# Front of a hybrid encoder kernel: six PSUM banks for projection outputs, evictions ahead of weight splits, split first transfers, and a gather of h with the norm's factor in the selection

## The chip, the cores and the metric

The kernel runs on one core of a Trainium2 chip. Its time is device microseconds of the whole execution; the time of a version is the median over runs, each with its own launch. TensorE is PE below (its weight loads are PEld), VectorE is DVE, ScalarE is ACT, GpSimd is POOL, and SyncE (SP) issues nearly all DMAs.

## The reference

One layer on 256 frames of width 1024, float32:

```
hn   = rmsnorm(h, g_mix);  proj = hn @ w_in            # 1024 -> 2048: u | B | C | v, 512 each
pool = (trailing mean of u over 2/4/8/16 frames - u) @ w_pool[g] * pool_scale
conv = B * causal_conv3(C * v)
h    = h + concat(pool, conv) @ w_out
h    = h + attention(rmsnorm(h, g_xattn) -> q, rmsnorm(mem, g_mem) -> k, v; 4 heads of 256) @ w_o
hn   = rmsnorm(h, g_moe);  logits = hn @ w_router + b_router
h    = h + sum over the top 4 of 32 experts e:
           gate * (((clip(lin) + 1) * swiglu(hn @ w_gate_up[e] + b)) @ w_down[e] + b)
out  = rmsnorm(h, g_final)
```

The expert weights are 12 MB for each of 32 experts; every expert is read.

## The kernel before

**Two parts.** The *front* is everything up to the routing; the *expert loop* follows. In the front each product is made of three passes in float32r: a weight chunk of 1 MB (`ring`, eight places) is taken as two *halves* of 128x1024; for half j ACT writes `w_hi[j % 4]` (`hi(j)`, a rounding copy), DVE writes `w_lo[j % 4]` (`lo(j)`, the remainder), and PE multiplies hi by hi, hi by lo and lo by hi. Both `hi(j)` and `lo(j)` wait until PE has finished half j-4 (`halves_used`). `project_rows` (w_v, w_out, w_o) is 12 matmuls of 128x512 for a half and puts its four row tiles in PSUM banks 2 to 5; `project_columns` and `project_u` (w_in, w_k, w_q) are 24 matmuls of 128x256 for a half.

**The order of the front** is written out by hand for each engine. PE: transposes of mem; w_v (halves 0 to 7, with the transposes of the normed x after the fifth and the seventh); u0, u1 (8 to 11), C0 (12, 13), v0 (14, 15), pool frames 0, C1 (16, 17), v1 (18, 19), pool product 0, pool frames 1, B0 (20, 21), pool product 1, B1 (22, 23); w_out (24 to 31); k0 to k3 (32 to 39); q0 to q3 (40 to 47) with the scores, the transposes of the probabilities (`turn_probs`) and the products with v (`attend`); w_o (48 to 55, `project_head`); transposes of h and the logits.

**Banks.** All outputs of columns, pool, keys, queries, scores and heads go through banks 0 and 1 in turn, in the order of the list `A_USES`; use n waits until use n-2 was evicted. Who evicts: u, C, the frames' differences d, the queries and the first copy of a head are ACT's, each behind the `hi` pair that stands before it; `conv_in(i)` on DVE multiplies v by C (`z_pad`) and then does six tap instructions, `pool_out(i)` four instructions (`mix_hi`, `mix_lo`), `gate_conv(i)` three, `keys_out(c)` one. Banks 6 and 7 serve transposes.

**The start.** ACT issues six small transfers of gain rows into `vec_rows`; PE transposes all 48 rows at once into `vec` before it transposes mem.

**The experts.** Eleven *slots* of 2 MB (`SLOT_ORDER`) hold the weights, six chunks for each expert: four of w_gate_up, two of w_down. The first eleven are loaded as the front gives up its memory, the last of them after the logits (`lg_full`). Chunk n from the twelfth on is issued by SP only when PE has used chunk n-10 counted from one (`chunks_used`). For expert s, PE multiplies the rows of the normed tokens `n_rows` (written by ACT at L981, columns reordered so that k of 8 goes with p) by the 0/1 matrix `sel` (`gather`), ACT copies the result to `xg_sb`, PE transposes it in four pieces (`turn_tokens`), DVE applies `gain_moe` (`tokens_out`), and then come gate_up, the activation, its transposes (`turn_act`, which read every fourth column), down and scatter. `add_back` adds the result to `h_rows`. `keep_clock(n)` is n matmuls of the identity with itself.

## Time and profile before

| | us |
|---|---|
| median of 3 runs | 1146.5 (1143.35 to 1148.73) |
| profiled execution, its own time | 1145.61 |
| its span | 1143.9 |
| PE busy | 1076.5 (94%) |
| DVE, ACT busy | 342.6, 197.7 |
| chain that ended last, PE / DMA / DVE | 63%, 25%, 8% |

The profiled execution lies 0.9 us under the median, and its span 1.7 us under its own time. The page cuts the span in 40 slices; from the tenth to the last but one the DMA engines move 426 to 430 GB/s, ahead of that less. Busy PE is no sign that PE is the limit: matmuls are pipelined, and what a stage waits for has to be read from its waits.

### The profile page before, as it was taken

To read this page: it belongs to the slowest core of one execution; us is meant where nothing else is said; L and a number is where in the kernel's file an instruction comes from. 1 tells how busy PE (TensorE), PEld (TensorE's weight loads), DVE (VectorE), ACT (ScalarE), POOL (GpSimd) and SP (SyncE) were. 2 spreads that over 40 slices of the span, in tenths; PEclk is the share of its full clock that TensorE was granted. 3 is DMA by queue.
4 is the path that set the end of the run, shared out by engine and by line. 5 is a ranking of instruction groups with operands and counts; after the bars stand their busy time and mean duration, and the time that the engine had idled before them with its cause. 6 is when DMAs were issued, how large, how long until landed. Compare 5 with 4: busy or idle time off the path is not lost.

```text
span 1143.9 us, 12842 instructions
## 1 busy us (share of the span) xinstructions
PE 1076.5 (94%) x5419; PEld 489.2 (43%) x5420; DVE 342.6 (30%) x573; ACT 197.7 (17%) x323; POOL 26.1 (2%) x53
## 2 busy tenths in 40 slices
PE   8979999999999999999999999999999989999995
PEld 7978997733333333333333333333332333333332
DVE  8555645312222222222222222222222212222223
ACT  6523544400000000000000110100000000000002
POOL 6200000000000000000000000000000000000000
PEclk9999999899999999999999999999999999999998
DMA  9964555789999999999999999999999999999993
GB/s 351 349 212 146 170 221 229 286 365 428 427 426 427 430 427 427 427 429 427 427 426 429 428 428 426 429 427 428 427 429 426 428 427 428 429 427 426 429 429 156
DMA packets 52007, 437.94 MB, mean 383 GB/s; under 512 B 5184, under 2 KB 23024, under 8 KB 27376
## 3 DMA queue, kind: packets, MB, share of 16 engines
q1 hardware_dynamic: 51856, 437.10, 92.0%
q8 instruction: 45, 0.74, 0.3%
q14 instruction: 10, 0.08, 0.0%
q10 hardware_dynamic: 96, 0.02, 0.0%
HBM read 435.47 MB, written 1.05 MB: 382 GB/s over the span
## 4 chain that ended last, share of the span: by engine, by line
PE 63%; DMA 25%; DVE 8%; ACT 2%; issue 1%; ACTq 0%; DVEq 0%
PE ps L734 26%; DMA slot<-in_w_gate_up 25%; PE ps L768 14%; PE ps L476 7%; PE ps L534 6%; PE ps L779 3%; PE ps L752 2%; DVE glu L1338 2%; DVE lin L1335 2%; DVE glu L1331 2%; DVE lin L1332 1%; ACT sig L824 1%; PE ps L499 1%; PE ps L723 1%; ACT w_hi L824 1%
## 5 line engine op out<-in xcount | busy, mean ns | idle before, releaser
L734 PE MATMUL ps<-slot,xT 128*64 128x512 f32 x2048 | 456.9, 595 | 17.2 <-DMA slot<-in_w_gate_up 16.4
L734 PEld LDWEIGHTS ps<-slot,xT 128*64 128x64 f32 x2048 | 142.0, 136 | 310.4 <-issue 266.1
L768 PE MATMUL ps<-slot,sig 128*64 128x512 f32 x1024 | 226.8, 595 | 8.0 <-ACT sig L824 8.0
L1344 DVE TENSOR_TENSOR h_rows<-ps,h_rows 128x1024 f32<-128x1024 f32 x64 | 75.4, 1219 | 368.3 <-PE ps L779 368.3
L768 PEld LDWEIGHTS ps<-slot,sig 128*64 128x64 f32 x1024 | 70.7, 137 | 143.6 <-issue 127.9
L995 ACT ACTIVATE sig<-glu 128x512 f32<-128x512 f32 x32 | 20.2, 632 | 546.3 <-DVE glu L1331 546.3
L1331 DVE TENSOR_SCALAR glu<-ps 128x512 f32<-128x512 f32 x32 | 22.1, 692 | 280.1 <-PE ps L734 280.1
L1093 DVE TENSOR_TENSOR w_lo<-ring,w_hi 128x1024 fp32r<-128x1024 f32 x56 | 68.2, 1225 | 74.7 <-ACT w_hi L824 74.6
L824 ACT ACTIVATE xg_sb<-ps 128x512 f32<-128x512 f32 x65 | 38.9, 598 | 245.3 <-PE ps L768 230.0
L824 ACT ACTIVATE w_hi<-ring 128x1024 fp32r<-128x1024 f32 x56 | 59.0, 1062 | 83.8 <-PE ps L476 52.3
L779 PE MATMUL ps<-xg_sb,g_sb 64*128 64x512 f32 x256 | 63.6, 615 | 0.7 <-ACT xg_sb L824 0.7
L708 PE MATMUL ps<-n_rows,sel 128*64 128x512 f32 x264 | 64.0, 607 | 0.0
L779 PEld LDWEIGHTS ps<-xg_sb,g_sb 64*128 64x128 f32 x256 | 22.0, 186 | 41.8 <-issue 40.2
L752 PE MATMUL ps<-ident,glu 128*128 128x128 f32 x128 | 23.9, 309 | 13.7 <-DVE glu L1338 13.7
L1325 DVE TENSOR_TENSOR xT<-ps,gain_moe 128x512 f32<-128x512 f32 x33 | 22.8, 691 | 44.3 <-PE ps L716 44.3
L708 PEld LDWEIGHTS ps<-n_rows,sel 128*64 128x64 f32 x264 | 19.2, 139 | 37.8 <-issue 37.7
L476 PE MATMUL ps<-hn_hi,w_hi 128*128 128x256 f32 x160 | 23.1, 287 | 6.9 <-DVEq L1166 3.1
L752 PEld LDWEIGHTS ps<-ident,glu 128*128 128x128 f32 x128 | 17.8, 208 | 23.2 <-DVE glu L1338 23.2
L824 ACT ACTIVATE sig<-ps 128x512 f32<-128x512 f32 x32 | 19.1, 598 | 31.9 <-PE ps L752 31.9
L476 PEld LDWEIGHTS ps<-hn_hi,w_hi 128*128 128x128 f32 x160 | 20.6, 191 | 8.1 <-DVEq L1166 3.3
L1335 DVE SCALAR_TENSOR_TENSOR lin<-lin,glu 128x512 f32<-128x512 f32 x32 | 22.1, 691 | 1.3
L1338 DVE TENSOR_TENSOR glu<-lin,sig 128x512 f32<-128x512 f32 x32 | 22.1, 692 | 1.1
(190 smaller groups left out, 708.8 us busy)
## 6 DMA issues: line engine op xcount, KB each, us to landing
slot<-in_w_gate_up SPq DMA_DIRECT2D x128, 2048.0 KB, 36.4
slot<-in_w_down SPq DMA_DIRECT2D x64, 2048.0 KB, 37.5
ring<-in_w_in SPq DMA_DIRECT2D x8, 1024.0 KB, 13.9
ring<-in_w_v SPq DMA_DIRECT2D x4, 1024.0 KB, 10.6
ring<-in_w_out SPq DMA_DIRECT2D x4, 1024.0 KB, 12.1
ring<-in_w_k SPq DMA_DIRECT2D x4, 1024.0 KB, 5.7
ring<-in_w_q SPq DMA_DIRECT2D x4, 1024.0 KB, 5.2
ring<-in_w_o SPq DMA_DIRECT2D x4, 1024.0 KB, 4.8
```

The lines of the kernel that those rows point to most:

```text
L476: mm = pe.matmul(bank[:, (j % 2) * SEQ:(j % 2 + 1) * SEQ], w[:, k, :], src[:, k, :], start=(n == 0 and k == 0), stop=(n == 2 and k == KC - 1),
L534: mm = pe.matmul(ps[:, bank_row[r], :], src[:, k, t * P:(t + 1) * P], w[:, half * HALF:(half + 1) * HALF], start=(n == 0 and k == 0), stop ...
L708: mm = pe.matmul(ps[CAP * half:CAP * (half + 1), bank_xg, :], sel[:, t, :], n_rows[:, t, half * HALF:(half + 1) * HALF], start=(t == 0), s ...
L734: mm = pe.matmul(ps[CAP * half:CAP * (half + 1), bank, :], lhsT, w[:, a * CHUNK + bank * D + half * HALF:a * CHUNK + bank * D + (half + 1) ...
L752: mm = pe.transpose(ps[:, bank_t[1], j * P:(j + 1) * P], act[:].rearrange("s (p r) -> s r p", r=4)[:, j, :], ident[:])
L768: mm = pe.matmul(ps[CAP * half:CAP * (half + 1), bank_y, :], lhsT, w[:, r * D + half * HALF:r * D + (half + 1) * HALF], start=False, stop= ...
L779: mm = pe.matmul(ps[:, (4 if t == 0 else 2) + half, :], g_sb[rws, t * P:(t + 1) * P], y_sb[rws, :], start=True, stop=True, skip_group_chec ...
L824: act_e.activation(dst, src, ACT.Copy).then_inc(done, 1)
L1093: dve.tensor_tensor(w_lo[j % LO_BUFS][:].rearrange("p (k n) -> p k n", **shape), src, w_hi[j % HI_BUFS][:].rearrange("p (k n) -> p k n", * ...
L1331: dve.tensor_scalar(glu[:], ps[:, 0, :], LIMIT, None, ALU.min).then_inc(glu_ok, 1)
L1335: dve.scalar_tensor_tensor(out=lin[:], in0=lin[:], scalar=1.0, in1=glu[:], op0=ALU.add, op1=ALU.mult).then_inc(step_link, 1)
L1344: dve.tensor_tensor(h_rows[:, t, :].rearrange("p (a n) -> p a n", a=2), ps[:, b:b + 2, :], h_rows[:, t, :].rearrange("p (a n) -> p a n", a ...
```

## The change

**Banks.** `A_BANK` gives each output one of six banks, 0 to 5; banks 2 to 5 are shared with the row tiles, so `FIRST_AFTER_ROWS` adds waits for the evictions of w_v and w_out, and the row products wait for the last use of their bank. **Order.** On ACT and DVE evictions move ahead of splits; the six taps of `conv_in` become `conv_taps`, which stands behind one more `lo`. **Start.** The gain of mem has its own small transfer and its own transpose, issued first; the other five are transposed after the third half of w_v. The first chunk of w_v comes in two transfers. DVE prepares 16 columns of the pooling band and no longer 256, POOL fills the rest. **Experts.** ACT's write of `n_rows` goes; `gather` reads `h_rows` with `sel_rstd`, which is `sel` times the factor of the norm, one DVE instruction of 128x128 more for each expert. The reordering of columns moves into the transposes of `xg_sb` (every fourth column) and into which rows of w_gate_up a chunk holds: 16 KB in a row for each partition as before, but 32 KB from partition to partition instead of 64 KB. `acc` is a sum apart from `h_rows`.

```diff
-A_USES = ["u0", "u1", "C0", "v0", "d0", "C1", "v1", "pool0", "d1", "B0", "pool1", "B1", "k0", "k1", "k2", "k3",
-          "q0", "q1", "s0", "q2", "s1", "q3", "s2", "s3", "o0", "o1", "o2", "o3", "logits"]
+A_BANK = dict(u0=0, u1=1, C0=2, v0=3, d0=0, C1=4, v1=5, pool0=1, d1=0, B0=2, pool1=3, B1=0, k0=1, k1=0, k2=2, k3=3,
+              q0=4, q1=5, s0=0, q2=1, s1=2, q3=3, s2=4, s3=5, o0=0, o1=1, o2=0, o3=1, logits=0)
+A_USES = list(A_BANK)
+FIRST_AFTER_ROWS = {"C0": 0, "v0": 1, "C1": 2, "v1": 3, "k2": 0, "k3": 1, "q0": 2, "q1": 3}
...
+def a_uses(bank, upto):
+
+    return sum(A_BANK[n] == bank for n in A_USES[:A_USES.index(upto) + 1])
...
+        acc, out_rows = n_rows, h_rows
...
+        def a_evicted(eng, name):
+
+            eng.wait_ge(a_free[A_BANK[name]], a_uses(A_BANK[name], name))
...
             if c < GATE_UP:
-                return w_gate_up[0, bass.ds(e, 1), :, :].rearrange("o (p k) n -> p (o k n)", k=KC)[:, BIG * c:BIG * (c + 1)]
+                rows_of = w_gate_up[0, bass.ds(e, 1), HALF * (c // 2):HALF * (c // 2 + 1), :].rearrange("o (p a) n -> p (o a) n", a=4)
+                return rows_of[:, 2 * (c % 2):2 * (c % 2 + 1), :].rearrange("p a n -> p (a n)")
...
+                if q == 0:
+                    sp.dma_start(dst[:, 0:1, :], src[:, 0:1, :]).then_inc(first_half_in, 16)
+                    dst, src = dst[:, 1:2, :], src[:, 1:2, :]
                 sp.dma_start(dst, src).then_inc(slot_full[q % FRONT_RING], 16)
...
                 project_rows("w_v", k, mn_hi, mn_lo)
+                if k == 2:
+                    pe.wait_ge(vec_in, 16 * 5)
+                    bank, done = t_begin("vec")
+                    pe.transpose(bank[:, 0:N_ROWS], vec_rows[:], ident[0:N_ROWS, 0:N_ROWS]).then_inc(done, 1)
...
             def gather(s):
-                pe.wait_ge(sel_ok, s + 1)
+                pe.wait_ge(sel_rstd_ok, s + 1)
...
-                        mm = pe.matmul(ps[CAP * half:CAP * (half + 1), bank_xg, :], sel[:, t, :],
-                                       n_rows[:, t, half * HALF:(half + 1) * HALF], start=(t == 0), stop=(t == TC - 1),
+                        mm = pe.matmul(ps[CAP * half:CAP * (half + 1), bank_xg, :], sel_rstd[:, t, :],
+                                       h_rows[:, t, half * HALF:(half + 1) * HALF], start=(t == 0), stop=(t == TC - 1),
...
             hi(1, 2, 3)
+            t_out("vec", lambda bank, done: copy(vec[:, 0:N_ROWS], bank[:, 0:N_ROWS], done))
+            act_e.wait_ge(t_free[1], t_use("vec")[1])
...
-            hi(16, 17)
+            hi(15, 16)
             a_out("C0", c_buf[:])
-            hi(18, 19)
+            hi(17, 18, 19)
             a_out("d0", dT[:, 0:2, :])
...
-            act_e.wait_ge(rstd_ok, 1)
-            for c in range(TC):
-                act_e.activation(n_rows[:, c, :].rearrange("t (k p) -> t k p", p=P),
-                                 h_rows[:, c, :].rearrange("t (p k) -> t k p", p=P), ACT.Copy,
-                                 scale=stat[:, 3, 2, c:c + 1]).then_inc(scaled, 1)
...
-            lo(16, 17, 18, 19)
-            conv_in(0)
-            lo(20, 21, 22, 23)
-            conv_in(1)
+            lo(16, 17, 18)
+            conv_product(0)
+            lo(19)
+            conv_taps(0)
+            lo(20, 21, 22)
+            conv_product(1)
+            lo(23)
             dve.wait_ge(bias_split, 2 * PARTS - 1)
             pool_out(0)
-            lo(24, 25)
+            lo(24)
+            conv_taps(1)
             gate_conv(0)
+            lo(25)
             pool_out(1)
-            lo(26, 27)
+            lo(26)
             gate_conv(1)
...
-            largest(0), lo(48, 49)
-            scale_probs(0), largest(1), lo(50)
-            turned(0), lo(51), scale_probs(1)
-            largest(2), largest(3), scale_probs(2), scale_probs(3)
+            largest(0), lo(48), scale_probs(0), lo(49)
+            largest(1), turned(0), scale_probs(1), lo(50, 51)
+            largest(2), scale_probs(2), largest(3), scale_probs(3)
...
+            def normalise_selected(s):
+
+                dve.wait_ge(sel_ok, s + 1)
+                rstd = stat[:, 3, 2, :].unsqueeze(2).broadcast_to([P, TC, CAP])
+                dve.tensor_tensor(sel_rstd[:], sel[:], rstd, ALU.mult).then_inc(sel_rstd_ok, 1)
```

What the change moves on ACT at the start, in the stage of w_v: these are its instructions from the first gain copy to the squares of mem, before:

```order
L824 ACTIVATE vec<-ps 128x48
L851 ACTIVATE mn_hi_61<-ps,vec 128x256 x4
L824 ACTIVATE w_hi0_89<-ring_49 128x1024
L851 ACTIVATE mn_hi_61<-ps,vec 128x256 x4
L824 ACTIVATE w_hi1_90<-ring_49 128x1024
L824 ACTIVATE w_hi2_91<-ring_49 128x1024
L824 ACTIVATE w_hi3_92<-ring_49 128x1024
L835 ACTIVATE squares_out_63,stat<-h_rows_83 128x1024 x2
L840 ACTIVATE stat<-stat,eps 128x2
L824 ACTIVATE w_hi0_89<-ring_49 128x1024
L824 ACTIVATE w_hi1_90<-ring_49 128x1024
```

And the same stretch of ACT after the change:

```order
L843 ACTIVATE vec<-ps 128x8
L870 ACTIVATE mn_hi_61<-ps,vec 128x256 x4
L843 ACTIVATE w_hi0_89<-ring_49 128x1024
L870 ACTIVATE mn_hi_61<-ps,vec 128x256 x4
L843 ACTIVATE w_hi1_90<-ring_49 128x1024
L843 ACTIVATE w_hi2_91<-ring_49 128x1024
L843 ACTIVATE w_hi3_92<-ring_49 128x1024
L843 ACTIVATE vec<-ps 128x40
L854 ACTIVATE squares_out_63,stat<-h_rows_83 128x1024 x2
L859 ACTIVATE stat<-stat,eps 128x2
L843 ACTIVATE w_hi0_89<-ring_49 128x1024
L843 ACTIVATE w_hi1_90<-ring_49 128x1024
```

A second copy of gains, of 40 rows, now stands between half 3 and the squares of x; half 4 (the next `w_hi0`) stands behind both.

DVE in the stage of w_in, from half 23 (`w_lo3`) to the gate product of B0 (`zc_74<-ps,zc_74`), before:

```order
L1093 TENSOR_TENSOR w_lo3_96<-ring_49,w_hi3_92 128x1024
L1125 TENSOR_TENSOR z_pad_73<-ps,c_buf_85 128x2x256
L1134 TENSOR_SCALAR zc_74<-z_pad_73,vec 128x256 x2
L1136 SCALAR_TENSOR_TENSOR zc_74<-z_pad_73,vec,zc_74 128x256 x4
L1162 TENSOR_SCALAR mix_hi_65<-ps,vec 128x256
L1163 SCALAR_TENSOR_TENSOR mix_lo_66<-ps,vec,mix_hi_65 128x256
L1162 TENSOR_SCALAR mix_hi_65<-ps,vec 128x256
L1163 SCALAR_TENSOR_TENSOR mix_lo_66<-ps,vec,mix_hi_65 128x256
L1093 TENSOR_TENSOR w_lo0_93<-ring_49,w_hi0_89 128x1024
L1093 TENSOR_TENSOR w_lo1_94<-ring_49,w_hi1_90 128x1024
L1152 TENSOR_TENSOR zc_74<-ps,zc_74 128x512
```

And after the change:

```order
L1140 TENSOR_TENSOR z_pad_73<-ps,c_buf_85 128x2x256
L1109 TENSOR_TENSOR w_lo3_96<-ring_49,w_hi3_92 128x1024
L1179 TENSOR_SCALAR mix_hi_65<-ps,vec 128x256
L1180 SCALAR_TENSOR_TENSOR mix_lo_66<-ps,vec,mix_hi_65 128x256
L1179 TENSOR_SCALAR mix_hi_65<-ps,vec 128x256
L1180 SCALAR_TENSOR_TENSOR mix_lo_66<-ps,vec,mix_hi_65 128x256
L1109 TENSOR_TENSOR w_lo0_93<-ring_49,w_hi0_89 128x1024
L1151 TENSOR_SCALAR zc_74<-z_pad_73,vec 128x256 x2
L1153 SCALAR_TENSOR_TENSOR zc_74<-z_pad_73,vec,zc_74 128x256 x4
L1169 TENSOR_TENSOR zc_74<-ps,zc_74 128x512
```

The product of v1 (`z_pad`) now stands ahead of half 23, the six taps behind the pool tiles and half 24, and half 25 behind the gate product.

DVE at the first selection, after the routing, before:

```order
L1291 SCALAR_TENSOR_TENSOR place<-ps,mask 128x2x32
L1310 TENSOR_TENSOR sel_104<-slot_no,place 128x128
L1311 COPY onehot0_107<-expert_id 96x64
L1281 SCALAR_TENSOR_TENSOR gate,small<-ex,mask 128x32 x2
L1284 RECIPROCAL small<-small 128x2
```

And after the change:

```order
L1314 SCALAR_TENSOR_TENSOR place<-ps,mask 128x2x32
L1333 TENSOR_TENSOR sel_104<-slot_no,place 128x128
L1334 COPY onehot0_107<-expert_id 96x64
L1340 TENSOR_TENSOR sel_rstd<-sel_104,stat 128x128
L1304 SCALAR_TENSOR_TENSOR gate,small<-ex,mask 128x32 x2
```

The gather waited for `sel`; it now waits for `sel_rstd`, two instructions later.

## Rows read from the trace of the kernel before

**Rows 1.** Busy time by stretch; the last columns are granted clock, DMA share, GB/s.

```profile
221.00:231.40 10.40, 10.14 (x46) 4.22 (x47) 3.71 (x20) 0.96 (x3) 0.00 (x0) 0.80 0.18 76
770.00:1116.00 346.00, 321.56 (x1504) 108.79 (x1502) 76.56 (x128) 30.90 (x57) 0.00 (x0) 1.00 1.01 428
```

**Rows 2.** Timeline of PE in the expert loop: start, duration, line; idle before, releaser.

```profile
722.78 3.60 PE L734 MATMUL ps<-slot,xT 128*64 128x512 f32 x16
750.38 3.60 PE L734 MATMUL ps<-slot,xT 128*64 128x512 f32 x16
...
1086.91 3.65 PE L734 MATMUL ps<-slot,xT 128*64 128x512 f32 x16 [1.24 <-DMA slot<-in_w_gate_up]
...
1116.29 3.65 PE L734 MATMUL ps<-slot,xT 128*64 128x512 f32 x16 [1.24 <-DMA slot<-in_w_gate_up]
```

**Rows 3.** Timeline of SP's queue, first issue after the eleven slots.

```profile
231.40 0.33 SPq L359 DMA_DIRECT2D slot<-in_w_down  x1
```

**Rows 4.** Timeline of the start.

```profile
2.88 0.38 ACTq L881 DMA_DIRECT2D vec_rows<-in_conv_w  x1
...
7.98 0.34 PE L546 MATMUL ps<-ident,vec_rows 48*128 48x48 f32 x1 [2.06 <-DMA vec_rows<-in_conv_w]
...
8.25 3.67 PE L448 MATMUL ps<-ident,mem_rows 128*128 128x128 f32 x16
```

**Rows 5.** Timeline of the w_v stage, to the first product of w_in.

```profile
16.21 1.09 ACT L835 ACTIVATE squares_out<-h_rows 128x1024 f32<-128x1024 f32 x1
...
21.09 1.07 PE L534 MATMUL ps<-w_hi,mn_hi 128*128 128x512 f32 x4
...
22.54 0.75 DVE L1063 TENSOR_SCALAR n_rows<-h_rows,stat 128x1024 f32<-128x1024 f32 x1
...
26.54 1.03 PE L448 MATMUL ps<-ident,n_rows 128*128 128x128 f32 x8
...
35.40 1.65 DVE L1080 SCALAR_TENSOR_TENSOR hn_lo<-ps,vec,hn_hi 128x256 fp32r<-128x256 f32 x4
...
37.16 1.19 PE L499 MATMUL ps<-w_hi,hn_hi 128*128 128x256 f32 x8 [0.48 <-issue]
```

**Rows 6.** Timeline of the w_in stage, PE's four waits (C1, frames 1, B0, B1).

```profile
63.85 1.00 PEld L476 LDWEIGHTS ps<-hn_hi,w_hi 128*128 128x128 f32 x8 [1.89 <-DVE z_pad L1125]
...
78.69 0.30 PEld L512 LDWEIGHTS ps<-band,u_rows 128*128 128x128 f32 x2 [2.61 <-issue]
...
83.36 1.02 PEld L476 LDWEIGHTS ps<-hn_hi,w_hi 128*128 128x128 f32 x8 [3.28 <-DVEq L1166]
...
92.39 1.01 PEld L476 LDWEIGHTS ps<-hn_hi,w_hi 128*128 128x128 f32 x8 [2.54 <-DVE zc L1152]
```

**Rows 7.** Timeline of the w_in stage, DVE: taps, a pool tile, the gate product.

```profile
79.37 1.80 DVE L1136 SCALAR_TENSOR_TENSOR zc<-z_pad,vec,zc 128x256 f32<-128x256 f32 x4
...
81.21 0.48 DVE L1162 TENSOR_SCALAR mix_hi<-ps,vec 128x256 fp32r<-128x256 f32 x1
...
91.65 0.68 DVE L1152 TENSOR_TENSOR zc<-ps,zc 128x512 f32<-128x512 f32 x1
```

**Rows 8.** Groups of instructions by line: busy us, mean ns, idle before.

```profile
L1093 DVE TENSOR_TENSOR w_lo<-ring,w_hi 128x1024 fp32r<-128x1024 f32 x56 | 68.2, 1225 | 74.7 <-ACT w_hi L824 74.6
...
L752 PE MATMUL ps<-ident,glu 128*128 128x128 f32 x128 | 23.9, 309 | 13.7 <-DVE glu L1338 13.7
...
L716 PE MATMUL ps<-ident,xg_sb 128*128 128x128 f32 x132 | 19.8, 273 | 0.0
```

**Rows 9.** Waits over the whole span: total us, times, longest.

```profile
PE ps L631 <- DVE probs L1221: 3.4, 3, 1.6
```

**Rows 10.** Timeline from the logits to the first gather.

```profile
215.19 4.25 ACT L981 ACTIVATE n_rows<-h_rows,stat 128x1024 f32<-128x1024 f32 x2
...
221.17 0.29 DVE L1310 TENSOR_TENSOR sel<-slot_no,place 128x128 f32<-128x128 f32 x1
...
221.61 3.68 PE L708 MATMUL ps<-n_rows,sel 128*64 128x512 f32 x8
```

More of the change, by code:

```diff
@@ L146, in program @@
         tri = sb("tri", [P, P])
+        sel_rstd = sb("sel_rstd", [P, TC, CAP])
         expert_id = sb("expert_id", [PARTS * E, E + 2], BF16)
@@ L194, in program @@
         bias_split = sem("bias_split")
-        a_full, a_free = sem("a_full"), [sem("a_free0"), sem("a_free1")]
+        a_full, a_free = sem("a_full"), [sem(f"a_free{i}") for i in range(6)]
         t_full, t_free = ([sem(f"{n}{i}") for i in range(4)] for n in ("t_full", "t_free"))
@@ L372, in _ @@
                     sp.wait_ge(end_out, 2 * c + half + 1)
-                    sp.dma_start(out[0, P * c:P * (c + 1), part], n_rows[:, c, part]).then_inc(stored, 16)
+                    sp.dma_start(out[0, P * c:P * (c + 1), part], out_rows[:, c, part]).then_inc(stored, 16)
             sp.wait_ge(stored, 16 * TC * 2)
@@ L412, in _ @@
                 step(pool.memset(later, 1.0 / w))
+                step(pool.memset(band[:, g, PAD:SEQ], 1.0 / w))
                 pool.wait_ge(counts_ok, g + 1)
@@ L458, in a_begin @@
             def a_begin(name):
-                n = a_use(name)
-                if n >= 2:
-                    pe.wait_ge(a_free[n % 2], n // 2)
-                return ps[:, n % 2, :]
+                bank = A_BANK[name]
+                before = a_uses(bank, name) - 1
+                if before:
+                    pe.wait_ge(a_free[bank], before)
+                if name in FIRST_AFTER_ROWS:
+                    pe.wait_ge(row_free if name[0] in "Cv" else h_added, FIRST_AFTER_ROWS[name] + 1)
+                return ps[:, bank, :]
             def split_half(j):
@@ L529, in project_rows @@
                         pe.wait_ge(w_lo_ok, j + 1)
-                    if k == 0 and n == 0 and bank_free is not None:
-                        pe.wait_ge(bank_free, r + 1)
+                    if k == 0 and n == 0 and last_use is not None:
+                        pe.wait_ge(a_free[bank_row[r]], a_uses(bank_row[r], last_use))
                     t, half = r % 2, r // 2
@@ L543, in _ @@
             keep_clock(9)
-            pe.wait_ge(vec_in, 16 * 6)
-            bank, done = t_begin("vec")
-            pe.transpose(bank[:, 0:N_ROWS], vec_rows[:], ident[0:N_ROWS, 0:N_ROWS]).then_inc(done, 1)
+            pe.wait_ge(mem_gain_in, 16)
+            bank, done = t_begin("vecm")
+            pe.transpose(bank[:, 0:KC], mem_gain_rows[:], ident[0:KC, 0:KC]).then_inc(done, 1)
             for c in range(TC):
@@ L715, in turn_tokens @@
                 for j in range(4):
-                    mm = pe.transpose(ps[:, bank_t[0], j * P:(j + 1) * P], xg_sb[:, j * P:(j + 1) * P], ident[:])
+                    mm = pe.transpose(ps[:, bank_t[0], j * P:(j + 1) * P], xg_sb[:].rearrange("s (p a) -> s a p", a=4)[:, j, :], ident[:])
                 mm.then_inc(xT_full, 1)
@@ L781, in scatter @@
                     mm.then_inc(sc_full, 1)
-            pe.wait_ge(scaled, 1 + TC)
             gather(0)
@@ L883, in _ @@
             fetch_table(ACT.Sqrt)
-            t_out("vec", lambda bank, done: copy(vec[:], bank[:, 0:N_ROWS], done))
+            t_out("vecm", lambda bank, done: copy(vec[:, ROW_MEM:ROW_MEM + KC], bank[:, 0:KC], done))
             act_e.wait_ge(t_free[1], 1)
@@ L1363, in _ @@
             prepare_and_activate(0, 1)
-            add_back(0)
+            add_back(0, before=h_rows)
             prepare_and_activate(1, 0)
```

114 lines of the change are left out of this document (58 added, 56 removed).

## The prediction

> **What bounds the kernel now.** I read the slices of the page first: DMA traffic is uneven for the first tenth of the slices and flat from there on, while PE is busy nearly throughout. So I asked for the stretches. From 770 to 1116 the DMA engines are full (share 1.01) at 428 GB/s, and just before the loop gets going, from 221 to 231.4, they stand at a share of 0.18 [rows 1]. Then the expert loop in PE's timeline: while chunks are in stock an expert takes 750.38 - 722.78 = 27.60 us; late in the loop it takes 1116.29 - 1086.91 = 29.38 us, and PE waits 1.24 us for a w_gate_up chunk [rows 2]. An expert is six chunks of 2.097 MB, and 12.58 MB at 428 GB/s is 29.4 us: late in the loop the transfers set the pace, and PE only used up the eleven slots' stock first. The supply starts when SP issues the first chunk beyond the stock, at 231.40 [rows 3], which is when PE has used its first chunk. From there 181 chunks follow without a hole, 181 x 4.90 = 887 us, to about 1118; the last arrival PE waits for is at 1116.29 [rows 2]. So
>
> end = (time of PE's first used chunk) + 887 us + a tail of 27.6 us (1143.9 - 1116.3).
>
> What the front saves ahead of that first chunk goes to the end one for one, since the engines are nearly idle just ahead of it: the eleven slots have landed by then, and their releases move with the front. What the change saves or adds inside the loop is worth nothing as long as an expert on PE stays under 29.4 us; it has 1.8 us to spare. The rest of the reading is therefore the front: where does PE wait, and for whom.
>
> **The start, term by term.** PE's first real work, the transpose of the gains, starts at 7.98 after 2.06 us of waiting for the sixth gain transfer, so PE was free at 5.92 [rows 4]. The sixth was issued at 2.88 and came 5.1 us later. The one transfer now awaited is issued first, about 0.8; with the same 5.1 us it is there at 5.9, and with any less, sooner. The transposes of mem then start 2.06 us earlier, and with them the whole chain of ACT and DVE to the first w_v half; DVE would have been in the way with its band reciprocals, which are now short. Half the first chunk is asked for where all of it was, so the transfer isn't late.
>
> But that gain is lost again. The other gains are transposed after the third half of w_v, and ACT must copy them before it squares x. PE leaves that half at 21.09 before [rows 5], so at 19.03 now; with transpose and copy ACT is free at about 19.4. Before, the squares of x began at 16.21 [rows 5]: ACT stands idle in between and its chain (squares, root, half 4, DVE's normed x) comes 3.2 us later than before. The normed x was ready at 22.54 + 0.75 = 23.3 and PE took it at 26.54 [rows 5]. It will be ready at 26.5: the slack is just used up. From there DVE must do six `lo` of 1.225 us [rows 8], eight tiles of 1.65 us for four [rows 5], and the statistics and diagonals of mem, about 1.5 us as an estimate from small instructions: 7.35 + 3.3 + 1.5 = 12.15, so 38.65, and u0 starts behind that. Before it started at 37.16, right behind the tiles' end at 37.05 [rows 5]: DVE waited on ACT in between then, and now it doesn't. The start is 1.5 us **later**, not 2.1 earlier.
>
> One unknown lies in this. The 16 transposes of mem took 3.67 us, 230 ns each, while eight of the same took 1.03 us later [rows 4, 5]: PE ran at its lower level, 1.2 GHz, in this stretch, after standing 2.06 us idle. That idle time goes. If the clock rises earlier, the transposes and the first half of w_v lose up to about 2 us, of which half lies beside mem's tiles on ACT; the third half then ends up to 1.1 us sooner, and all behind it. Bounds: the start costs 0.4 to 1.5 us; I take **0.8 lost**, nearer the low end, because PE is now busy without a break. The Trainium skill, "TensorE: Matmul & The Clock Gate", Part 1, says that the array runs at half rate until it has been busy for a while, with a phase that varies from run to run; by that rule the loss would be near 0.4, by the row taken as it stands 1.5.
>
> **The w_in stage.** PE waits four times for evictions in banks 0 and 1: 1.89, 2.61, 3.28 and 2.54 us, 10.32 together [rows 6]. With six banks C1 and both pool products find their bank free; u, C and d are evicted one split earlier, well ahead of need. Both weight splits of a half (ACT 1.1, as for the square of the same shape [rows 5]; DVE 1.225 [rows 8]) fit into the 2.9 us that PE takes for it, and four buffers let them run up to three halves ahead. What is late next is the end of DVE's queue. Without the first three waits (7.8 us) B0 ends at 81.4 on the old clock, and PE comes to w_out at 88.0. DVE: half 24 can't be split before B0's first half is used, 2.9 ahead of 81.4, so hi is done at 79.8 and lo at 81.0; six taps, 2.45 (1.80 for four [rows 7]), 83.5; the gate product with its two followers, 1.9 (first 0.68 [rows 7]), 85.4; lo(25), 86.6; four pool instructions of 0.48 [rows 7] with their links, 88.7. The second row tile of w_out sits in bank 3, which this last eviction frees. PE waits 0.7 us there. Net **9.6 gained**. Below that I can think of a further miss of one split (2.3); above, of the 0.7.
>
> **The scores.** PE waits three times for the scaled probabilities, 3.4 us [rows 9]. The scaling now stands ahead of the next split: the first two waits, 1.6 each, vanish. At the end of the stage both engines run through their queues with PE waiting: following each instruction, the third and the fourth scaling come 0.6 and 0.7 us late. Net **2.1 gained**, between 1 and 3.4.
>
> **From the logits to the first chunk.** ACT's 4.25 us for the reordered normed rows [rows 10] end at 219.4, and the gather begins at 221.61 behind `sel` (221.17 to 221.46 [rows 10]): the removed work lay beside PE's clock-keeping matmuls and the ranks, and gives nothing. `sel_rstd` is added on the path: 0.29 for an instruction of its size, behind the one-hot copy, about **0.4 lost**. The transposes of `xg_sb` read every fourth column; `turn_act` does so now, 309 ns against 273 [rows 8], so **0.15 lost** once on the path. In the loop this adds 0.15 and the DVE instruction, which lies in time that DVE waits for PE; the 1.8 us to spare cover both. The new layout of w_gate_up keeps the 16 KB runs: no change. Were PE's cover gone, each 0.1 us per expert would cost 3.2 us.
>
> **Sum.** -0.8 + 9.6 + 2.1 - 0.4 - 0.15 = 10.35 us gained, on the profiled execution's own time: 1145.6 - 10.35 = 1135.25. This lies 0.9 under the median of the runs, so 1136.1 for a median; I say 1136. Half a per cent, 5.7 us, is about what these runs can tell from no change, with 1143.4 to 1148.7 for one and the same kernel.
>
> **The rivals.**
> *The start keeps its gain.* If the gain copy isn't in the way of ACT (PE reaches it much earlier, or there is more slack behind), the 2.06 us stay: 1136.1 - 2.9 = 1133.2. Against it: ACT's idle time follows from the order alone. 0.13.
>
> *Evictions ahead of splits block the queues.* An eviction waits for PE's last matmul of a unit; the split behind it then starts that late, and PE waits for a split where it waited for a bank. Each such miss costs up to 1.1 + 1.2 = 2.3 us; two of them in w_in or the scores make 1140.7. For it: ACT waits for PE before most splits already. Against it: four buffers are 8.6 us of stock. 0.13.
>
> *The supply hides it.* The loop's start moves, but the last of the eleven slots land later than needed, or the chunks' queue has been behind since before 231.4: then the end stays at 1146. The share of 0.18 [rows 1] speaks against it: the engines would have to be full there. 0.04.
>
> *The new rows of w_gate_up load slower* (the side that ends slower). Two thirds of the 887 us are w_gate_up. Today its 64 KB pitch and w_down's 16 KB pitch run within the same 428 GB/s [rows 1], so a pitch between the two should as well. The gain is gone when those chunks are 1.8% slower (10.35 / 591), and from 2.8% on the kernel is slower by over half a per cent; at 5% it would be 1136 + 30 = 1166. The same 18 us stand against any growth of an expert on PE past 29.4. The Trainium skill, "DMA: Bandwidth & Descriptors", table of latency and other measured facts, gives rows at large powers of two apart as slow, 207 GB/s at 512 KB; by that rule the pitch to fear is the larger, and this change halves it. No run here shows such a pitch. 0.06.
>
> *The forecast* has 0.64, with its own range 1133 to 1139.
>
> **Range and chances.** The range reaches over the first two rivals: 1131 to 1141; about two in ten is left out. Faster by over 0.5% is under 1140.8: the forecast, the first rival and half the second, 0.83. Within 0.5%: the rest of the second, the third and part of the fourth, 0.12. Slower: 0.05.
>
> **What the profile would show.** PE's first mem transposes at about 6.2; ACT idle from about 14 to 19 ahead of a `vec` copy; u0 at 37.5 to 38.7; the three `z_pad` and `band` waits gone, and a wait of under 1 us at the second matmul of w_out, near 89; waits on the probabilities of about 1.3 in all; the first issue beyond the stock at 221; an expert late in the loop still at 29.4, with waits for w_gate_up; a tail of 27.6. The prediction is wrong if the late period differs from 29.4, if the supply has holes, or if PE's waits in w_in show a split (`w_hi`, `w_lo`) as releaser.

## The result, and the profile after

The changed kernel takes 1128.57 us, median of 4 runs (1128.38 to 1128.86); the kernel before takes 1145.1 us, median of 4 (1143.35 to 1148.73). The ratio is 0.9852, 95% interval 0.9825 to 0.9879: 1.5% faster. The prediction was 1136.0 with a range of 1131 to 1141; the sign was right, the time lies 2.4 us below the range. The two profiled executions took 1145.61 and 1128.38 us: 17.2 us gained where 10.35 were worked out.

I follow the gain along PE's timeline, as the lead of the kernel after over the one before at each landmark. The start first; columns are start, duration, engine and line, shape, and in brackets the idle time before with its releaser:

```profile
5.90 1.95 PE L464 MATMUL ps<-ident,mem_rows 128*128 128x128 f32 x16
9.29 1.16 PE L552 MATMUL ps<-w_hi,mn_hi 128*128 128x512 f32 x4 [1.44 <-ACT w_hi L843]
...
17.94 0.20 ACT L843 ACTIVATE vec<-ps 128x40 f32<-128x40 f32 x1 [4.49 <-PE ps L578]
18.17 1.06 ACT L854 ACTIVATE squares_out<-h_rows 128x1024 f32<-128x1024 f32 x1
...
21.79 1.17 PE L552 MATMUL ps<-w_hi,mn_hi 128*128 128x512 f32 x4 [0.94 <-ACT w_hi L843]
...
25.20 1.09 PE L464 MATMUL ps<-ident,n_rows 128*128 128x128 f32 x8 [0.42 <-DVE n_rows L1079]
...
25.17 2.36 DVE L1109 TENSOR_TENSOR w_lo<-ring,w_hi 128x1024 fp32r<-128x1024 f32 x2
...
34.97 1.65 DVE L1096 SCALAR_TENSOR_TENSOR hn_lo<-ps,vec,hn_hi 128x256 fp32r<-128x256 f32 x4
...
36.73 1.19 PE L518 MATMUL ps<-w_hi,hn_hi 128*128 128x256 f32 x8 [0.48 <-issue]
```

The transposes of mem start 2.35 us earlier and take 1.95 us for the 3.67 of [rows 4], 122 ns each for 230: by these durations TensorE is at its upper level by then. ACT stands idle for 4.49 us ahead of the second gain copy, as predicted, and the squares of x begin at 18.17 for 16.21 in [rows 5]. What is left at u0 is a lead of 37.16 - 36.73 = 0.43 us.

The w_in stage after: the first matmuls of C1, B0 and B1, which had their waits in [rows 6], and of w_out:

```profile
61.48 1.20 PE L495 MATMUL ps<-hn_hi,w_hi 128*128 128x256 f32 x8
...
75.17 1.20 PE L495 MATMUL ps<-hn_hi,w_hi 128*128 128x256 f32 x8
...
81.69 1.30 PE L495 MATMUL ps<-hn_hi,w_hi 128*128 128x256 f32 x8
...
87.63 0.39 PE L552 MATMUL ps<-w_hi,mix_hi 128*128 128x512 f32 x1
88.31 0.97 PE L552 MATMUL ps<-w_hi,mix_hi 128*128 128x512 f32 x3 [0.29 <-DVEq L1183]
```

No product has an idle time in front. The last pool eviction (DVE) holds w_out's second matmul for 0.29 us, the place that the prediction named with 0.7. A matmul of these takes 0.23 us (four from 98.24 to 99.17 before), so had the wait stood ahead of w_out's first matmul, w_out would begin at 88.31 - 0.23 = 88.08, 0.45 later than it does. It began at 98.24 before: counted so, the lead is 10.16, and the stage brought 9.73.

The scores, where [rows 9] had three waits:

```profile
167.91 0.63 PE L652 MATMUL ps<-ident,probs 128*128 128x128 f32 x4 [0.37 <-DVE probs L1246]
...
170.91 0.63 PE L652 MATMUL ps<-ident,probs 128*128 128x128 f32 x4 [0.65 <-DVE probs L1246]
171.42 1.20 PE L552 MATMUL ps<-w_hi,hn_hi 128*128 128x512 f32 x4
```

Two waits of 1.0 us in all are left, for 3.4. The first w_o matmul, now at 171.42, was at 184.10 before: the lead is 12.68, 0.13 having been lost between w_out and the first query (144.87 before, 134.84 after), so the scores brought 2.65.

Then the part behind w_o. Before and after, PE alone, from the transposes of h to the first gate_up matmul; before:

```profile
209.47 1.04 PE L671 MATMUL ps<-ident,h_rows 128*128 128x128 f32 x8
...
212.85 3.26 PE L680 MATMUL ps<-wr_sb,gT 128*128 128x32 f32 x24
215.92 3.76 PE L456 MATMUL ps<-ident 128*128 128x128 f32 x16
...
227.70 3.65 PE L734 MATMUL ps<-slot,xT 128*64 128x512 f32 x16
```

After, with DVE's added instruction and SP's first issue beyond the stock among them:

```profile
196.81 1.03 PE L691 MATMUL ps<-ident,h_rows 128*128 128x128 f32 x8
...
202.80 2.03 PE L472 MATMUL ps<-ident 128*128 128x128 f32 x16
...
206.31 0.29 DVE L1340 TENSOR_TENSOR sel_rstd<-sel,stat 128x128 f32<-128x128 f32 x1
...
206.65 1.94 PE L728 MATMUL ps<-h_rows,sel_rstd 128*64 128x512 f32 x8 [0.60 <-DVE sel_rstd L1340]
...
214.73 0.33 SPq L374 DMA_DIRECT2D slot<-in_w_down  x1
```

The first gate_up matmul of after stands at 211.04. From h's transposes to it the kernel before needs 18.23 us, the one after 14.23. The same 16 clock-keeping matmuls take 3.76 and 2.03 us, the same 8 gather matmuls 3.68 [rows 10] and 1.94. The stretches' granted clock (sixth column after the stretch's length, in front of the DMA share) says why; before:

```profile
214.90:225.20 10.30, 10.30 (x41) 7.47 (x40) 3.81 (x27) 6.40 (x8) 0.00 (x0) 0.50 0.67 255
```

After, that stretch, one over w_in, and the expert loop:

```profile
214.90:225.20 10.30, 10.30 (x50) 3.45 (x48) 0.08 (x1) 0.00 (x0) 0.00 (x0) 1.00 0.92 359
80.00:100.00 20.00, 19.71 (x114) 17.28 (x114) 15.64 (x23) 7.05 (x7) 0.00 (x0) 1.00 0.54 176
201.00:211.00 10.00, 9.18 (x68) 6.91 (x67) 4.74 (x29) 4.11 (x7) 0.00 (x0) 1.00 0.83 318
770.00:1100.00 330.00, 306.12 (x1430) 104.57 (x1428) 74.17 (x132) 29.65 (x55) 0.00 (x0) 1.00 1.01 428
```

In the execution profiled before, TensorE ran at the lower level (1.2 GHz) for 10.3 us around the gather; after it ran at 2.4 GHz from 201 to 211. The lead at the first gate_up matmul is 16.66, and SP's first issue has moved from 231.40 [rows 3] to 214.73, 16.67. The loop takes it over one for one: an expert late in the loop still takes 1099.65 - 1070.28 = 29.37 us at 428 GB/s, as in [rows 1, 2]:

```profile
1070.28 3.65 PE L754 MATMUL ps<-slot,xT 128*64 128x512 f32 x16 [1.25 <-DMA slot<-in_w_gate_up]
...
1099.65 3.65 PE L754 MATMUL ps<-slot,xT 128*64 128x512 f32 x16 [1.24 <-DMA slot<-in_w_gate_up]
```

So the ledger of the profiled pair is 0.43 (start) + 9.73 (w_in) - 0.13 + 2.65 (scores) - 0.02 + 4.00 (from the logits on) = 16.66, and 0.57 more to the end, against -0.8, +9.6, +2.1 and -0.55 predicted. The term to explain is the last, the 4.00 from the logits on.

The 0.57 lies behind the loop. From SP's first issue beyond the stock to the end of PE's last wait for a chunk both executions take 884.9 us; from that wait to the end of the span it is 27.6 us before and 1126.6 - 1099.65 = 26.95 after. In the profiled executions of this document the span ends 915.5 to 915.7 us after the first gate_up matmul wherever the new start is in the kernel (seven), and 915.9 to 916.5 wherever the old one is (seven). So these 0.6 us go with the start's edits; why, no run here shows.

### The profile page after: what moved, and what is told of

It is laid out like the page before. It is cut to its first block, busy times and chain, and to the rows that moved or that the text cites. A ratio compares the mean times of both kernels' runs of the same rounds, so it can differ in the third digit from the quotient of the medians.

```text
span 1126.6 us, 12882 instructions
## 1 busy us (share of the span) xinstructions
PE 1071.1 (95%) x5420; PEld 486.9 (43%) x5421; DVE 341.2 (30%) x606; ACT 193.1 (17%) x322; POOL 24.9 (2%) x57
## 4 chain that ended last, share of the span: by engine, by line
PE 62%; DMA 25%; DVE 9%; ACT 2%; issue 1%; DVEq 0%; POOL 0%; POOLq 0%; ACTq 0%
PE ps L754 27%; DMA slot<-in_w_gate_up 25%; PE ps L788 15%; PE ps L495 6%; PE ps L552 5%; PE ps L799 3%; PE ps L772 2%; DVE lin L1363 2%; DVE glu L1366 2%; DVE glu L1359 2%; DVE lin L1360 1%; ACT sig L843 1%; PE ps L518 1%; PE ps L743 1%; PE ps L472 1%
## 5 line engine op out<-in xcount | busy, mean ns | idle before, releaser
L1372 DVE TENSOR_TENSOR n_rows<-ps,n_rows 128x1024 f32<-128x1024 f32 x62 | 73.0, 1220 | 355.5 <-PE ps L799 355.5
L728 PE MATMUL ps<-h_rows,sel_rstd 128*64 128x512 f32 x264 | 62.3, 592 | 0.6 <-DVE sel_rstd L1340 0.6
L728 PEld LDWEIGHTS ps<-h_rows,sel_rstd 128*64 128x64 f32 x264 | 18.9, 137 | 37.8 <-issue 37.1
L495 PE MATMUL ps<-hn_lo,w_hi 128*128 128x256 f32 x160 | 22.5, 283 | 0.0
```

The source lines that it names most:

```text
L495: mm = pe.matmul(bank[:, (j % 2) * SEQ:(j % 2 + 1) * SEQ], w[:, k, :], src[:, k, :], start=(n == 0 and k == 0), stop=(n == 2 and k == KC - 1),
L728: mm = pe.matmul(ps[CAP * half:CAP * (half + 1), bank_xg, :], sel_rstd[:, t, :], h_rows[:, t, half * HALF:(half + 1) * HALF], start=(t == ...
L1372: dve.tensor_tensor(acc[:, t, :].rearrange("p (a n) -> p a n", a=2), ps[:, b:b + 2, :], before[:, t, :].rearrange("p (a n) -> p a n", a=2) ...
```

## The experiments

Theory A: the clock. Removing PE's waits in w_in does two things: it gives back the waits themselves, and it keeps the TensorE at its upper level, which the kernel before loses now here, now there. Theory B: the gather's edits shorten the part behind the logits, or keep the level up there. The kernel before ran again beside each group of experiments, with medians of 1143.89 (23 runs, e1), 1144.03 (23, e2) and 1144.45 us (17, e3), altogether 1140.7 to 1148.66 with a median of 1143.98. Against that the changed kernel's gain is 15.4 us.

**Each part alone.** The three parts of the diff shown with the change, each put alone into the kernel before.

> The kernel before with the six banks and the new order of evictions and splits alone (old start, old gather). The sum of the prediction has 9.6 + 2.1 us for it; the two traces show 9.7 in the stage of w_in and 2.65 in the scores. Theory A (the 4 us beyond the sum come from PE's clock, which was at half rate from 214.9 to 225.2 in the profiled execution of before and is not a property of the gather): about 1133 where the granted clock falls after the logits, about 1129 where it does not, so runs of two kinds. Theory B (the change of the gather keeps the clock up): all near 1133, with the low stretch in each.

> The kernel before with the new start alone (separate gain of mem, two first transfers, short band). Both theories: u0 starts 0.4 us sooner, so 0.4 us faster than before and not to be told from it; under theory A single runs may lie 4 us apart, by whether the clock falls after the logits.

> The kernel before with the gather of h alone (factor in the selection, no reordered copy of the normed rows, new rows of w_gate_up). Theory A: 0.5 us slower than before in runs of the same clock. Theory B: 3.5 to 4 us faster in every run, and the granted clock after the logits stays at 1.0.

Measured: only banks and order 1129.8 us (1129.51 to 1130.91), ratio 0.9876 (0.9855 to 0.9897). Only the start 1143.7 (1141.13 to 1146.64), ratio 0.9996 (0.9982 to 1.0009). Only the gather 1144.16 (1141.69 to 1148.89), ratio 1.0004 (0.999 to 1.0018). Six banks with the new order give 14.1 of the 15.4 us by themselves; the other two parts alone give nothing that can be told. The two kinds of runs that theory A expected of the first didn't come: all four lie near 1129.8, none near 1133. Theory B falls: with the gather's edits and the old banks the level is lost just as before. The windows of that execution (1148.37 us), with the granted clock ahead of the DMA share:

```profile
8.00:20.00 12.00, 11.02 (x44) 8.91 (x45) 10.73 (x16) 10.76 (x20) 10.90 (x18) 0.72 1.03 401
80.00:88.00 8.00, 5.11 (x23) 4.68 (x24) 4.32 (x11) 0.60 (x1) 0.00 (x0) 0.57 0.42 133
...
216.00:228.00 12.00, 11.81 (x57) 9.20 (x56) 4.23 (x30) 4.00 (x7) 0.00 (x0) 0.57 0.74 285
```

The execution with only the start (1143.58 us) had 0.79 in 80 to 88 and in 92 to 100, and 1.00 behind the logits. What each loss costs can be read between the landmarks: from u0 to w_out the kernel before takes 98.24 - 37.16 = 61.08 us with 1.00 throughout, the execution with only the gather 62.49, the one with only the start 64.06; from h's transposes to gate_up they take 18.40 and 14.30. So the place of the loss changes from one execution to another, and with it the time. Over the 63 runs of the kernel before, the 29 with a mean granted clock of 0.994 or more have a median of 1143.35 us, the 16 with 0.990 or less one of 1147.9. The Trainium skill, "TensorE: Matmul & The Clock Gate", Part 1, says that the gate's phase varies from run to run; that the 63 runs of this one program have mean clocks from 0.986 to 0.997 agrees with it.

The only-banks kernel shows besides what the gather's edits take away at the upper level. ACT and PE there:

```profile
203.05 4.19 ACT L990 ACTIVATE n_rows<-h_rows,stat 128x1024 f32<-128x1024 f32 x2
...
207.29 1.94 PE L718 MATMUL ps<-n_rows,sel 128*64 128x512 f32 x8 [0.80 <-ACT n_rows L990]
```

When TensorE is fast, ACT's scaled rows are what the gather waits for, 0.80 us; the changed kernel waits 0.60 for `sel_rstd` in their place.

**The waits filled instead of removed.** In the kernel before, dummy matmuls ahead of the four waits in w_in, each lot shorter than its wait; nothing is evicted sooner.

```diff
+            pe.wait_ge(row_free, 4)
+            keep_clock(6)
             project_columns("C1", hn_hi, hn_lo)
...
+            keep_clock(9)
             pool_frames(1)
+            keep_clock(11)
             project_columns("B0", hn_hi, hn_lo)
...
+            keep_clock(8)
             project_columns("B1", hn_hi, hn_lo)
```

> The kernel before, with dummy 128-column matmuls (6, 9, 11 and 8 of them, 0.25 us each at the high level) put ahead of PE's four waits in the w_in stage; each lot is shorter than its wait, so no wait gets shorter in wall time and no work moves. Theory A (the waits cost twice: their own 10 us, and the clock level that TensorE loses behind them): the level stays up in the w_in stage, median 1141.5 to 1142.5 against 1143.9, runs closer together, granted clock 0.995 or more in most. Theory B (the waits cost only their own length and the level falls for a reason of its own): 1143.9 with the same scatter of 5 to 7 us. If the dummies are in the way, 1145 or more, with PE reaching B0 later than before.

Measured: 1141.41 us (1140.93 to 1143.04, 12 runs) against 1144.03 (1140.7 to 1148.16, 23 runs), ratio 0.9981 (0.997 to 0.9992). Theory A holds in the median and in the spread: 2.6 us come back (0.9 to 3.4 by the interval) although no transfer or eviction has been moved, and the runs spread over 2.1 us where the kernel before spreads over 7.5. It doesn't hold in the clocks: 0.995 or more was expected in most runs, and three of twelve have it. The profiled execution (0.994) still had 0.79 in 4 to 12 us. Its timeline, PE:

```profile
75.49 2.17 PE L456 MATMUL ps<-ident 128*128 128x128 f32 x18
77.88 0.67 PE L512 MATMUL ps<-band,u_rows 128*128 128x256 f32 x2 [0.23 <-DVE z_pad L1130]
...
97.39 1.09 PE L534 MATMUL ps<-w_hi,mix_hi 128*128 128x512 f32 x4
...
208.63 1.03 PE L676 MATMUL ps<-ident,h_rows 128*128 128x128 f32 x8
...
222.95 8.37 PE L739 MATMUL ps<-slot,xT 128*64 128x512 f32 x38
```

The frames that waited 2.61 us before [rows 6] wait 0.23 behind the dummies. From u0 (36.31) to w_out it takes 61.08 us, to the hundredth what the kernel before took in its profiled execution: there the level never fell in w_in, so the filling changed nothing in that stage, and this pair of traces differs in the start (0.85 us) and behind the logits. From h's transposes to gate_up it takes 222.95 - 208.63 = 14.32 us with the old gather at the upper level; the changed kernel took 14.23. So of the 4.00 us, 3.91 are the clock level and 0.09 the edits.

**A filler too many.** As before, and 11 dummies also in the way from w_o to the transposes of h.

```diff
+            for _ in range(11):
+                pe.matmul(ps[:, 1, 0:P], ident[:], ident[:], start=True, stop=True)
             pe.wait_ge(h_added, 6)
             transpose_frames(0), transpose_frames(1)
```

> As the kernel with the four filled waits, and 11 dummies also ahead of the wait for the w_o evictions (209.6 to 213 us in the profile before). Theory A (idle stretches of some us take the level down, wherever they lie): the level stays up after the logits too, another 1 to 2 us, 1140 to 1141.5, all runs within 2 us. Theory B: 1143.9, scatter as before. If the low stretch after the logits has another cause than that wait (the routing steps behind it, in which PE mostly stands), the level is still lost there in some runs and this kernel equals the one with four filled waits.

Measured: 1143.42 us (1142.76 to 1145.53, 12 runs), 2.0 slower than with four filled waits. I had read a wait into that place that isn't there:

```profile
208.35 2.62 PE L690 MATMUL ps<-ident 128*128 128x128 f32 x22
210.80 1.04 PE L676 MATMUL ps<-ident,h_rows 128*128 128x128 f32 x8
```

The dummies run from 208.35 and the transposes follow at once; in the kernel before they stood right behind w_o at 209.47, without idle time. The dummies cost 2.4 us of PE. They may bring a little: seven of the twelve runs have a mean clock of 0.997 or more, where one had with four filled waits, and the median rose by 2.0 only. But even the three best, at 0.998, took 1142.76 to 1142.85. Taken alone this run doesn't tell the theories apart.

**The start filled too.** Four filled waits, and the clock-keeping ahead of the gains' transpose from 9 to 13.

> The kernel before with the four filled waits of w_in (1141.4 in the earlier call against 1144.0) and 4 more dummies ahead of the transpose of the gains, which waits 2.1 to 2.5 us for a transfer. If idle time of TensorE is what takes the level down, the stretch of the first 20 us stays up as well: 1140 to 1141, runs within 1 us, granted clock 0.997 or 0.998. If the low stretch at the start has another cause, it equals the kernel with four filled waits, with clocks of 0.994 and some runs at 1143.

Measured: 1140.6 us (1140.12 to 1144.63, 12 runs; eight of them within 1140.12 to 1140.64), ratio 0.9964 (0.9946 to 0.9981) to 1144.45. The median came in as expected, the spread did not: four runs at clocks of 0.996 and 0.992 lie up to 4 us above. Its start, u0, and the first matmuls of w_out and w_o:

```profile
8.04 0.26 PE L546 MATMUL ps<-ident,vec_rows 48*128 48x48 f32 x1 [1.27 <-DMA vec_rows<-in_conv_w]
8.23 1.97 PE L448 MATMUL ps<-ident,mem_rows 128*128 128x128 f32 x16
...
35.96 1.19 PE L499 MATMUL ps<-w_hi,hn_hi 128*128 128x256 f32 x8 [0.48 <-issue]
...
97.02 1.09 PE L534 MATMUL ps<-w_hi,mix_hi 128*128 128x512 f32 x4
...
182.90 1.17 PE L534 MATMUL ps<-w_hi,hn_hi 128*128 128x512 f32 x4
```

The transposes of mem begin where they began in [rows 4] and take 1.97 us, not 3.67; u0 comes at 35.96, 1.2 us sooner. The old start at the upper level is thus 36.73 - 35.96 = 0.77 us ahead of the new one. Behind the logits this execution (1141.84 us) lost the level all the same: 0.92 in 215 to 229, and 15.39 us from h's transposes to gate_up for 14.32.

**Banks against order.** The changed kernel with one of the two taken back: the six banks with ACT's and DVE's queues in their old order, and two banks in turn with the queues in their new order. Of the second, the mapping and the wait of the rows:

```diff
+A_BANK = {n: i % 2 for i, n in enumerate(A_USES)}
...
-                        pe.wait_ge(a_free[bank_row[r]], a_uses(bank_row[r], last_use))
+                        pe.wait_ge(bank_free, r + 1)
```

> The changed kernel with its six banks, but ACT's and DVE's queues in the old order (two splits, then an eviction; scaling of the probabilities behind a split). Banks give nearly all of w_in: three of the four waits need only a free bank, so 1129 to 1132: 0.7 to 2 us later in w_in, 1.6 in the scores. If the order carried half of the 9.7 us of w_in, 1133 to 1136.

> The changed kernel with two banks in turn, and only the new order of evictions and splits. Each of the three waits for a bank shrinks by the one split (1.1 to 1.2 us) that stood ahead of the eviction, and the scores keep their 2.6: 12.4 - 9.7 + 3.5 = 6 us better than before at most, 1138 to 1140, with waits of 1 to 2 us left in w_in and the clock scattering as before. If the banks alone matter, 1141 to 1143.

Measured: new banks with the old order 1130.65 us (1130.46 to 1130.91), old banks with the new order 1136.39 (1134.73 to 1136.7). Beside six banks the order is worth 2.1 us, and all of it in the scores: w_out begins at 87.92 there, in one piece and 0.16 ahead of the changed kernel although u0 came 0.29 later, and among PE's waits up to 235 us stands, as before,

```profile
PE ps L652 <- DVE probs L1238: 3.4, 3, 1.6
```

With two banks the order is worth 7.6 us in the median, more than the 6 I had allowed. Two waits for a bank are left:

```profile
78.02 2.00 PE L496 MATMUL ps<-hn_hi,w_hi 128*128 128x256 f32 x8 [1.93 <-DVEq L1184]
...
88.22 1.97 PE L496 MATMUL ps<-hn_hi,w_hi 128*128 128x256 f32 x8 [1.81 <-DVE zc L1170]
```

and behind each the first eight matmuls take 2.0 us where they take 1.2 at the upper level (granted clock 0.53 to 0.61 in 78 to 82 and 0.55 to 0.59 in 88 to 92, 1.00 around them). Here the level falls right behind a wait, and it costs: B0 takes 7.36 us to the pool product behind it (85.38 - 78.02) for the 5.86 of before, and B1 7.35 us to w_out for 5.85. So of PE's four waits, 9.2 us by the matmuls' rows, 3.7 are left, but from u0 to w_out the time falls only from 61.08 to 58.48 us. The banks alone take it to 50.90. Less than a third of the gain comes from w_in: in the profiled execution the lead over the kernel before at gate_up is 8.7, of which 2.6 lie in w_in, 2.0 from w_out to w_o, and 4.0 behind the logits, where the clock was 1.00. In w_in the banks and the order work on the same waits: the banks remove them all, the order more than half, and both together bring no more than the banks alone.

**The start and the gather beside six banks.** The changed kernel without the edits of the start, and without those of the gather.

> The changed kernel without the edits of the start (six banks and order, gather of h with the factor in the selection). Only six banks ran at 1129.8. The prediction charged 0.55 us for the gather's edits: then 1130.3. The trace of only six banks says otherwise: there the gather waits 0.80 us for ACT's scaled rows, 1.18 us from the last mask matmul to the gather, where the changed kernel takes 0.99, so the edits are worth +0.15: 1129.6.

> The changed kernel without the gather's edits (six banks and order, and the start). By the traces the start is worth 0.5 us beside six banks (u0 at 36.73 against 37.27) and the gather 0.15: 1128.7 to 1129.2. By the prediction's terms (start -0.8) it would be slower than only six banks: 1130.6.

Measured: without the start 1130.2 us (1129.42 to 1131.72, clocks 0.992 to 0.998), without the gather 1129.12 (1128.15 to 1129.21). The second says that the gather's edits are worth 0.5 and the start 0.7; the first that the start is worth 1.6 and the gather nothing. The profiled run without the start (1131.72) had a granted clock of 0.79 in 4 to 20 us and 0.88 in 201 to 215, with no wait in w_in. Together with the traces this is a small gain for each, the start's being its lead at u0 and the 0.6 us behind the loop; the size of the gather's edits I leave between 0.4 lost and 0.5 gained by the medians, with 0.09 gained by the traces. The 1130.2 lies nearer to the 1130.3 of the prediction's terms than to the 1129.6 that I expected, but only one of its six runs has a clock above 0.996, so it doesn't bear the prediction's -0.55 out.

**The second gain copy out of ACT's way.**

```diff
-            t_out("vec", lambda bank, done: copy(vec[:, 0:N_ROWS], bank[:, 0:N_ROWS], done))
-            act_e.wait_ge(t_free[1], t_use("vec")[1])
             for c in range(TC):
...
             root_of(2)
+            t_out("vec", lambda bank, done: copy(vec[:, 0:N_ROWS], bank[:, 0:N_ROWS], done))
+            act_e.wait_ge(t_free[1], t_use("vec")[1])
             hi(6, 7, 8)
```

> The changed kernel, with ACT's second copy of gains moved behind the two squares of x, halves 4 and 5 and the squares of mem. If ACT's idle 4.5 us ahead of that copy hold up the w_v stage, as the prediction's start term says, PE's waits for half 4 (0.94), the normed x (0.42) and the tiles vanish, u0 starts near 34 instead of 36.7, and the kernel is 2.5 to 3 us faster than the changed one: 1125.7. If the stage waits for its transfers instead, nothing changes: 1128.5.

Measured: 1126.25 us (1125.91 to 1127.18, 5 runs), ratio 0.9842 (0.9824 to 0.986) to the kernel before: 2.3 us better than the changed kernel, and the best of all. ACT squares x in the time that it stood idle, and u0 follows 2.6 us sooner than after:

```profile
13.42 1.09 ACT L854 ACTIVATE squares_out<-h_rows 128x1024 f32<-128x1024 f32 x1
...
23.55 1.03 PE L464 MATMUL ps<-ident,n_rows 128*128 128x128 f32 x8
...
34.13 1.19 PE L518 MATMUL ps<-w_hi,hn_hi 128*128 128x256 f32 x8 [0.45 <-issue]
```

**Fewer dummies after the logits.** On top of the last, to trim what is left; the first expert's one-hot copy also moves behind `sel_rstd`.

```diff
-            keep_clock(8)
+            keep_clock(6)
             pe.wait_ge(masked, TC)
```

> The changed kernel with the second gain copy behind the squares (1126.25 alone), 6 clock-keeping matmuls in place of 8 after the logits, and the first expert's one-hot copy behind sel_rstd. The copy is worth 0.1; the two dummies nothing at the high level (the mask isn't ready sooner) and 0.9 us at the low one, in which one of five runs was: 1126.0 to 1126.2, at most 1126.8 for a single run. If fewer dummies let the level fall ahead of the gather, 1127 to 1129.

Measured: 1127.61 us (1126.29 to 1129.52, 5 runs, clocks 0.993 to 0.998), 1.4 more than with eight; it ran beside a kernel before of 1144.45, the other beside one of 1143.89. Its trace has the second thing that I had written down, though the level falls as the gather begins and not ahead of it (granted clock 1.00 in 200 to 204, 0.57 in 204 to 208):

```profile
200.29 1.58 PE L472 MATMUL ps<-ident 128*128 128x128 f32 x12
202.25 0.41 PE L715 MATMUL ps<-mask,tri 128*128 128x32 f32 x2 [0.37 <-DVE mask L1298]
...
204.15 3.63 PE L728 MATMUL ps<-h_rows,sel_rstd 128*64 128x512 f32 x8 [0.60 <-DVE sel_rstd L1342]
```

The gather takes 3.63 us for 1.94. With eight dummies, too, the profiled run (clock 0.995) had a granted clock of 0.66 in 200 to 205, and its sixteen clock-keeping matmuls took 3.60 us, while three of its five runs had 0.998, and here one. That the two missing dummies are the cause is not shown.

The runs of all these kernels together say how far theory A reaches. With six banks, and so without the waits in w_in, 34 runs of seven kernels have mean clocks from 0.992 to 0.998; the kernel before has 0.986 to 0.997. Without the waits less is lost, but the low stretches don't vanish: behind the logits three of the seven profiled executions with six banks took 15.67, 15.67 and 15.93 us for the 14.2 to 14.3 of the others, where the kernel before took 18.23.

## Why the prediction was wrong

**What bounds the kernel** was right. The lead at PE's first used chunk, 16.66 us, went to the end; the supply ran without a hole at 428 GB/s, 884.9 us before and after for the 887 worked out, and the late period stayed at 29.4. Only the tail was 26.95 and not 27.6. The rivals of a hiding supply and of slower rows of w_gate_up fall with it, and so does the one of blocked queues: in w_in no wait has a split as its releaser.

**The start** was forecast as 0.8 lost, between 0.4 and 1.5, and shows 0.43 gained, outside of these bounds. The mechanism was right: ACT's 4.49 us of idle time ahead of the copy, and 2.3 us back in the median once the copy is moved. Two sizes were not. DVE's chain behind the normed x was put at 12.15 us and ran from 25.17 to 36.62, 11.45; the change costs 0.77 at one and the same level (36.73 against 35.96), where the working has 1.5. And the level, for which the prediction allowed up to 1.1 and in effect took 0.7, brought 37.16 - 35.96 = 1.20. That the measured 0.77 stands so near the 0.8 forecast is chance, since the 0.8 already had part of the level's gain in it. PE isn't busy without a break either: it waits 1.44 us ahead of w_v.

**w_in** was 9.73 for 9.6, **the scores** 2.65 for 2.1. Both terms held, the scores within their bounds of 1 to 3.4. The rival of a start that keeps its gain, 1133.2, is answered by the experiments: the order of ACT's queue took 2.3 us, and moving one copy gives them back.

**From the logits to the first chunk** is where the prediction failed. It took the durations of [rows 10], the gather's 3.68 us and what lies ahead of it, as fixed, and priced the edits alone; but these were durations at the lower clock level (0.50 in 214.9 to 225.2); the same gather takes 1.94 us at the upper one. 3.91 us of the 4.00 gained here are the level. The prediction did look at the level, but at one place only (mem's transposes), and never asked in which executions, and for how long, it falls elsewhere. The -0.55 for the edits was wrong by itself, by 0.6 us: at the upper level ACT's scaled rows are what the gather waits for, and they weren't beside other work as I had read at the lower one.

How much is the clock in the medians: filling the waits with dummies, in w_in and at the start, brings 1144.45 down to 1140.6, 3.85 us (2.2 to 6.2 by the interval); from there to 1128.57 there are 12.0 us left, the removed waits. The prediction's terms, measured against the trace with start and waits filled, are -0.77 for the start, (97.02 - 35.96) - (88.08 - 36.73) = 9.71 for w_in, and (182.90 - 97.02) - (171.42 - 88.08) = 2.54 for the scores; behind the logits that trace lost the level, and the trace with four filled waits gives 0.09. Together they are 11.6, and 12.1 with the 0.57 behind the loop. So the change has two gains of about 12 and 4 us, of which the first was predicted at 10.35, and the second not at all. For the profiled pair it is 11.57 + 1.20 (level at the start) + 3.91 (level behind the logits) + 0.57 = 17.25, for the 17.2 measured.

The time lies 7.4 us below the forecast. 2.4 of these are no error of the gain: the prediction put the median 0.9 us above its profiled execution by three runs, and over 63 runs it lies 1.6 below it, at 1144.0. The other 5.1 are the gain, 15.4 for 10.35, with the level as the largest part. The margin of 2.4 us below the range is less than the level's 3.85; had the base been 1144.0, the time would still have been at the edge.

What isn't settled: why a run loses the level at the start or behind the logits when the waits lie in w_in. Where the level falls in w_in, it falls right behind a wait. For the other two places only the filled kernel's median and spread, and the clocks of the kernels with six banks, show that they are tied to those waits; no trace shows how, 110 us apart.

## What to carry to other kernels

Before a stretch's durations enter a sum, read its granted clock: where it is below 1.00, two prices exist for it (here 18.23 and 14.32 us for the same work), and a change that removes idle time of TensorE may make the dearer one rarer. A spread of runs that follows the mean clock is the sign to look for. Dummy matmuls that fill a wait tell its clock share from its length, by the medians of many runs of one more kernel. Where two cures work on the same wait (more banks, earlier evictions), don't add them up: price each beside the other, and read from a trace in which stage each brings its part.
